# Hybrid decoder step: prompt attention in the block order 0, 1, 7, 6, 5, 4, 3, 2, with each selection mask made one block ahead

## The chip, the cores and the metric

The kernel runs on one core of a Trainium2 chip. The metric is the device time of one execution in microseconds, median of several runs.

## What is computed

One step of a two-layer decoder trunk (d = 1024) for a prompt of 1024 tokens and a sample group of 8 sequences of 4 tokens with 1024 tokens of past. Layer 0 is a recurrent mixer (RG-LRU and gated DeltaNet) with an MLP, layer 1 is sparse attention with an MLP. The change lies in the sparse attention of the prompt, in the reference:

```python
def blk(args):                      # one block of 128 queries
    q_b, qi_b, wi_b, bi = args
    tpos = bi * qb + jnp.arange(qb)
    sc = index_scores(qi_b, wi_b, ki)
    sc = jnp.where(kpos[None, None, :] <= tpos[None, :, None], sc, -jnp.inf)
    _, idx = lax.top_k(sc, topk)    # 256 keys for each query
    valid = idx <= tpos[None, :, None]
    return sparse_attend(q_b, k[bidx, idx], v[bidx, idx], valid)

o = lax.map(blk, (blocks(q), blocks(qi), blocks(wi), jnp.arange(nb)))   # 8 blocks
```

There are 8 query heads on 2 key heads. A block may only look back, so block i sees 128 (i + 1) keys; blocks 0 and 1 see at most 256 keys and need no selection. The blocks do not depend on each other.

## The kernel before

The program is written by hand, engine by engine, and the order of each engine is that of the code; semaphores join them. Selected keys are not gathered. Instead the index scores of blocks 2 to 7 and of the samples stay in SBUF (`sc`, `sc_s`), a bitwise search finds each row's 256th largest score, and a mask of 0 and -1e30 over all keys (`mb` for the prompt, `mb_s` for the samples) is added to the attention scores.

`mask(q)` (line 1156) makes one mask on VectorE in five instructions as wide as the block: equal to the limit, a running count of the equals, the equals that still fit into the quota, those above the limit, and the scaling to bf16 (lines 1160 to 1164). Each waits for the one before. Masks 0 to 5 belong to blocks 2 to 7 (384 to 1024 columns), mask 6 to the samples (32 partitions, 1056 columns). The last instruction counts up `mask_r`.

The prompt's attention goes over 16 groups, two for each block, one for each key head: group n has block n // 2. A group has four heads.

- PE, `scores(n)` (line 709): for each head the product of queries and keys, and a product of the identity with the mask that adds it in PSUM. There are two places in PSUM for heads, so the third head waits until the exponential of the first is done. A group of blocks 2 to 7 waits for its mask by `mask_r`.
- VectorE, `head_max` (line 1172): row maximum of each head (line 1169) and its scaling.
- ScalarE, `exps(n)` (line 927): exponentials of the four heads into `pr`, with the sums of the rows.
- VectorE, `normalise(n)` (line 1184): reciprocal and product, four times.
- PE, `values(n)` (line 738): for each tile of 128 keys four transposes (line 747) and, one tile later, the product with the values (line 753). Between them the transposed tile is copied to `ptt`: the first tile of a group by VectorE (line 1204), the others by ScalarE (`ptt_copies`, line 938).
- VectorE, `output(n)` (line 1179): copies the result of a group to `oq` (line 1182).

PE takes scores(n + 1) ahead of values(n). VectorE's loop over n is, in this order: the four maxima of group n + 1, the ptt copy of group n, the output of group n - 1, the normalising of group n + 1, and for n below 7 mask n. At n = 7 stands a copy of the sample queries (`qs`, line 1212), whose memory the masks use as scratch.

Behind the 16 groups comes the sample stage. SyncE loads the pages of past keys and values for it: the key pages of the first four sequences early, then (`rest_of_sync`, line 581) it waits for all seven masks and loads the value pages of sequences 0 and 1; the value pages of sequences 2 and 3 wait for the end of all 16 groups, and the rest follows as buffers come free.

Of the kernel before, what the change touches and what calls it, by code (L numbers as in the profile page):

```python
# [22 lines left out]
P = 128  # L23
# [7 lines left out]
QB = SEQ // P  # L31
# [18 lines left out]
KV = 2  # L50
# [135 lines left out]
def build(nc, A, O):  # L186

    ctx = ExitStack()
    with ctx:
# [321 lines left out]
        HEADS = GROUPS * GRP  # L511
        steps_before = [sum(k // KV + 1 for k in range(n)) for n in range(GROUPS + 1)]

# [85 lines left out]
        def rest_of_pe(pe, unit, first_unit, norm_sum, mlp):  # L599
# [110 lines left out]
            def scores(n):  # L710
                i, kv = n // KV, n % KV
                if i >= 2:
                    pe.wait_ge(S["mask_r"], i - 1)
                for g in range(GRP):
                    a = n * GRP + g
                    if a >= 2:
                        pe.wait_ge(S["at_exp"], a - 1)
                    for k, (c0, cn) in enumerate(cuts(P * (i + 1))):
                        bank = 2 * (a % 2) + k
                        pe.matmul(ps[:, bank, 0:cn], oq[:, GRP * kv + g, i * P:(i + 1) * P], oq[:, 8 + kv, c0:c0 + cn],  # L720
                                  start=True, stop=False, skip_group_check=True)
                        if i < 2:
                            mm = pe.matmul(ps[:, bank, i * P:(i + 1) * P], id_b[:, :], bias_b[:, :], start=False, stop=True,
                                           skip_group_check=True)
                        else:
                            mm = pe.matmul(ps[:, bank, 0:cn], id_b[:, :], mb[:, sc_off[i] + c0:sc_off[i] + c0 + cn],
                                           start=False, stop=True, skip_group_check=True)
                    mm.then_inc(S["at_mm"], 1)
# [9 lines left out]
            def values(n):  # L738
                i, kv = n // KV, n % KV
                pe.wait_ge(S["at_nrm"], GRP * (n + 1))  # L740
# [97 lines left out]
        def rest_of_act(act, own, norm_root, square_unit, mlp):  # L838
# [88 lines left out]
            def exps(n):  # L927
                w = P * (n // KV + 1)
                for g in range(GRP):
# [8 lines left out]
            def ptt_copies(n):  # L938
                for k in range(1, n // KV + 1):
                    c = steps_before[n] + k  # L940
                    act.wait_ge(S["at_tr"], c + 1)
                    if c >= 2:
                        act.wait_ge(S["at_pv"], c - 1)
                    act.activation(ptt[:, c % 2, :], ps[:, 4 + c % 2, :], ACT.Copy).then_inc(S["at_ptt"], 1)
# [52 lines left out]
        def rest_of_dve(dve, own, norm_mean, output_units, mlp):  # L997
# [157 lines left out]

            def mask(q):
                s, m, pn, w = rows_of[q]
# [6 lines left out]
                dve.tensor_scalar(m, pre, -1.0, -MASKED, ALU.add, ALU.mult).then_inc(S["mask_r"], 1)  # L1164
                dve.wait_ge(S["mask_r"], q + 1)

# [5 lines left out]
            def head_max(a):  # L1172
                if a < HEADS:
                    dve.wait_ge(S["at_mm"], a + 1)
                    if a >= 4:
                        dve.wait_ge(S["at_exp"], a - 3)
                    maximum(a, bank2(2 * (a % 2), P * (a // (GRP * KV) + 1)))

            def output(n):
                i, kv = n // KV, n % KV  # L1180
                dve.wait_ge(S["at_pv"], steps_before[n + 1])
                dve.tensor_copy(oq[:, GRP * kv:GRP * (kv + 1), i * P:(i + 1) * P], quad(6 + n % 2)).then_inc(S["at_o"], 1)

            def normalise(n):
                w = P * (n // KV + 1)
                for g in range(GRP):
# [9 lines left out]
            for n in range(GROUPS):  # L1196
# [10 lines left out]
                if n + 1 < GROUPS:  # L1207
                    normalise(n + 1)
                if n < NB:
                    mask(n)  # L1210
                if n == NB:
                    dve.tensor_copy(qs[:, :, :, :].rearrange("p b h t -> p h b t"),
# [1345 lines left out]
```

## Time and profile before

| | |
|---|---|
| median of 3 runs | 3252.92 us (3252.11 to 3254.89) |
| the profiled execution, its own time | 3254.98 us |
| its span | 3253.2 us |
| PE (matmul) busy | 2950.3 us, 91% |
| VectorE (DVE) busy | 1403.7 us, 43% |
| ScalarE (ACT) busy | 749.3 us, 23% |
| GpSimd (POOL) busy | 936.0 us, 29% |
| mean granted TensorE clock | 0.935 |

PE is TensorE's products, PEld its weight loads, SPq the DMA issues of SyncE. Times in the trace are microseconds from the start of the span. The granted clock is the share of TensorE's full clock (2.4 GHz) that the chip grants it; 0.5 is 1.2 GHz, and a value between the two is a mean over a stretch that had both. The 16 groups lie between some 1940 and 2189 us, the sample stage between 2189 and 2337 us; the MLPs of the two layers, which make up most of the span, lie in front and behind.

### The profile page before, as it was taken

The page shows a single profiled execution, that of the slowest core. Times are in us where ns is not written, and L with a number is a line of the kernel's source. Part 1 is how long each engine was busy: PE and PEld are TensorE (multiplying, and loading weights), DVE is VectorE, ACT ScalarE, POOL GpSimd, SP SyncE. Part 2 cuts the span into 40 slices and gives each one's busy share as a digit, 9 for nine tenths or more (in the row PEclk, how much of TensorE's full clock was granted, in tenths as well). Part 3 has the DMA queues.
Part 4 walks back from the last instruction along what each step waited for, and adds up shares of the span by engine and source line. Part 5 has one row for each costly group of instructions (what it writes and reads, how often), then busy time and mean ns, then how long its engine had stood idle before and what let it go on. Part 6 is the DMA issues. An engine that isn't in the chain of part 4 may idle for free.

```text
span 3253.2 us, 43038 instructions
## 1 busy us (share of the span) xinstructions
PE 2950.3 (91%) x17384; PEld 2735.1 (84%) x17393; DVE 1403.7 (43%) x1868; ACT 749.3 (23%) x1158; POOL 936.0 (29%) x561
## 2 busy tenths in 40 slices
PE   5989899978899999999989946898798999999996
PEld 5889779968899999999977933446698999999995
DVE  6568266653422222212568887531134222222225
ACT  3353323320200011100235552332202100001111
POOL 2334223303343333334321310000032344333331
PEclk8999989969999999999999967997699999999998
DMA  4112100012111111111311120003210111111111
GB/s 146 39 33 60 29 26 1 1 57 71 30 48 47 45 39 42 45 45 48 107 38 37 46 82 1 26 10 105 83 45 26 46 49 45 48 40 42 42 44 66
DMA packets 237233, 153.09 MB, mean 47 GB/s; under 512 B 21243, under 2 KB 232884, under 8 KB 236169
## 3 DMA queue, kind: packets, MB, share of 16 engines
q1 hardware_dynamic: 226000, 121.17, 13.1%
q10 hardware_dynamic: 11116, 30.33, 2.6%
q8 instruction: 77, 1.26, 0.2%
q14 instruction: 40, 0.33, 0.0%
HBM read 133.46 MB, written 18.01 MB: 47 GB/s over the span
## 4 chain that ended last, share of the span: by engine, by line
PE 78%; DVE 13%; ACT 6%; issue 1%; DMA 0%; ACTq 0%; DVEq 0%
PE ps L1435 59%; ACT junk L898 3%; PE ps L720 2%; PE ps L789 2%; PE ps L753 2%; PE ps L1602 1%; PE ps L1587 1%; PE ps L1606 1%; DVE hl L2512 1%; DVE uc L2165 1%; PE ps L822 1%; PE ps L1512 1%; DVE mx L1169 1%; PE ps L747 1%; DVE cnt L1124 1%
## 5 line engine op out<-in xcount | busy, mean ns | idle before, releaser
L1331 POOL TENSOR_TENSOR w_hi<-w_raw,ones 128x512 fp32r<-128x512 f32 (+1 forms) x250 | 373.5, 1494 | 2023.9 <-PE ps L1435 1908.9
L1435 PE MATMUL ps<-xh,w_hi 128*128 128x352 f32 x2928 | 645.6, 329 | 68.1 <-DVE xl L2463 23.4
L1435 PE MATMUL ps<-xl,w_hi 128*128 128x352 f32 x2928 | 636.3, 326 | 0.0
L1435 PE MATMUL ps<-xh,w_lo 128*128 128x352 f32 x2928 | 635.4, 325 | 0.0
L1435 PEld LDWEIGHTS ps<-xh,w_hi 128*128 128x128 f32 x2928 | 505.0, 191 | 76.8 <-issue 63.2
L1435 PEld LDWEIGHTS ps<-xh,w_lo 128*128 128x128 f32 x2928 | 507.3, 189 | 0.0
L1435 PEld LDWEIGHTS ps<-xl,w_hi 128*128 128x128 f32 x2928 | 503.0, 190 | 0.0
L1334 POOL TENSOR_TENSOR w_lo<-w_raw,w_hi 128x512 fp32r<-128x512 f32 (+1 forms) x250 | 491.9, 1968 | 19.6
L2528 DVE TENSOR_TENSOR x<-x,ps 128x1056 f32<-128x1056 f32 x128 | 160.6, 1254 | 502.0 <-PE ps L1435 502.0
L2063 ACT ACTIVATE hs<-hu 128x1056 f32<-128x1056 f32 x64 | 69.7, 1090 | 1253.4 <-DVE hu L2504 1253.4
L1435 PE MATMUL ps<-hh,w_hi 128*128 128x352 f32 x1536 | 333.2, 325 | 13.7 <-DVE hl L2512 13.7
L1435 PE MATMUL ps<-hh,w_lo 128*128 128x352 f32 x1536 | 331.1, 323 | 0.0
L1435 PE MATMUL ps<-hl,w_hi 128*128 128x352 f32 x1536 | 330.5, 323 | 0.0
L2504 DVE SCALAR_TENSOR_TENSOR hu<-ps,rstd 128x1056 f32<-128x1056 f32 x64 | 80.5, 1258 | 560.4 <-PE ps L1435 560.0
L1435 PEld LDWEIGHTS ps<-hh,w_hi 128*128 128x128 f32 x1536 | 260.9, 189 | 17.9 <-ACT hh L2065 17.9
L1435 PEld LDWEIGHTS ps<-hh,w_lo 128*128 128x128 f32 x1536 | 263.4, 188 | 0.0
L1435 PEld LDWEIGHTS ps<-hl,w_hi 128*128 128x128 f32 x1536 | 261.0, 188 | 0.0
L720 PE MATMUL ps<-oq 128*128 128x512 f32 (+3 forms) x192 | 91.1, 569 | 68.5 <-ACT pr L935 51.1
L720 PEld LDWEIGHTS ps<-oq 128*128 128x128 f32 x192 | 39.0, 223 | 104.2 <-ACT pr L935 60.8
L1368 POOL TENSOR_TENSOR dn_lo<-dn_lm,cst 128x512 f32<-128x512 f32 (+1 forms) x49 | 67.4, 1410 | 189.6 <-ACT dn_lm L1984 189.6
L2512 DVE TENSOR_TENSOR hl<-hs,hh 128x1056 fp32r<-128x1056 f32 x64 | 115.1, 1810 | 7.2 <-DVE hu L2504 4.2
L2165 DVE SCALAR_TENSOR_TENSOR uc<-ub,prm,uc 128x1080 f32<-128x1080 f32 x48 | 94.1, 1960 | 25.5 <-ACT uc L1813 24.3
(374 smaller groups left out, 3035.6 us busy)
## 6 DMA issues: line engine op xcount, KB each, us to landing
w_raw<-in_w_up SPq DMA_DIRECT2D x64, 512.0 KB, 4.1
w_raw<-in_w_down SPq DMA_DIRECT2D x128, 256.0 KB, 2.7
w_raw<-in_w_in_rec SPq DMA_DIRECT2D x24, 512.0 KB, 3.9
x_spill<-x ACTq DMA_DIRECT2D x2, 4224.0 KB, 12.8
x<-x_spill ACTq DMA_DIRECT2D x4, 2112.0 KB, 7.6
w_raw<-in_w_in_att SPq DMA_DIRECT2D x16, 512.0 KB, 3.8
kpg<-in_cache_k SPq DMA_DIRECT2D x64, 128.0 KB, 2.0
vpg<-in_cache_v SPq DMA_DIRECT2D x64, 128.0 KB, 2.0
```

Source lines behind the costliest of these rows:

```text
L720: pe.matmul(ps[:, bank, 0:cn], oq[:, GRP * kv + g, i * P:(i + 1) * P], oq[:, 8 + kv, c0:c0 + cn], start=True, stop=False, skip_group_check ...
L753: pe.matmul(ps[:, 6 + n % 2, :], vtok[:, k - 1, kv * P:(kv + 1) * P], ptt[:, (c - 1) % 2, :], start=k == 1, stop=k == i + 1).then_inc(S["a ...
L898: ins = act.activation(junk[0:pn, junk_off[q]:junk_off[q] + w], s, ACT.Sign, scale=-1.0, bias=trial[0:pn, q:q + 1].bitcast(F32), accum_out ...
L1331: pool.tensor_tensor(w_hi[:, j % 2, 0:n], w_raw[:, j % 2, 0:n], ones[:, 0:1].to_broadcast([P, n]), ALU.mult).then_inc(w_hi_done, 1)
L1334: pool.tensor_tensor(w_lo[:, j % 2, 0:n], w_raw[:, j % 2, 0:n], w_hi[:, j % 2, 0:n].bitcast(F32), ALU.subtract).then_inc(w_split, 1)
L1368: pool.tensor_tensor(dn[f"lo{l}"][c % 2][0:w, :, 0:w], dn["lm"][0:w, :, 0:w], cst[0:w, C_LEVEL + l:C_LEVEL + l + 1, 0:w].to_broadcast([w, ...
L1435: mm = pe.matmul(ps[:, 3 * (j % 2) + t, 0:n], w[:, j % 2, k * P:(k + 1) * P], r[:, k, c0:c0 + n], start=(k == 0 and p == 0), stop=(k == kt ...
L2063: act.activation(hs[:, q % 2, :], hu[:, q % 2, :], ACT.Square).then_inc(S["hsq_r"], 1)
L2165: ins = dve.scalar_tensor_tensor(uc[:, 0:UB - 3], ub[:, i:i + UB - 3], prm[:, at_w:at_w + 1], uc[:, 0:UB - 3], ALU.mult, ALU.add)
L2504: dve.scalar_tensor_tensor(hu[:, q % 2, :].rearrange("p (a t) -> p a t", a=3), set_view(first + q, 0, 3)[:, :, 0:352], 0.0, r3, ALU.max, A ...
L2512: dve.tensor_tensor(hl[:, q - 1, :], hs[:, (q - 1) % 2, :], hh[:, q - 1, :].bitcast(F32), ALU.subtract)\
L2528: dve.tensor_tensor(xm, xm, set_view(j, 0, 3)[:, :, 0:352], ALU.add).then_inc(set_free, 1)
```

## The change

A table `BLOCKS` gives the block of each pair of groups: 0, 1, 7, 6, 5, 4, 3, 2. All that depended on n // 2 as the block's number now asks `block_of(n)`: widths, offsets, and the count of tiles ahead of a group (`steps_before`). Masks are made in the order in which the blocks come (`MASKS`: 5, 4, 3, 2, 1, 0, then the samples), and `mask_after` says behind which n of VectorE's loop each stands: the mask of block 7 behind n = 0, then one behind the first group of each block for the block that follows, and the samples' behind n = 13. The copy of the sample queries moves from n = 7 to n = 14. Line numbers grow by 7 or 8 behind the table.

```diff
--- before.py
+++ after.py
@@ -509,7 +509,14 @@
         w_out_att = A["w_out_att"][0].rearrange("(k p) n -> p k n", p=P)
         GROUPS = QB * KV
         HEADS = GROUPS * GRP
-        steps_before = [sum(k // KV + 1 for k in range(n)) for n in range(GROUPS + 1)]
+        BLOCKS = [0, 1] + list(range(QB - 1, 1, -1))
+        MASKS = [i - 2 for i in BLOCKS[2:]] + [NB - 1]
+        mask_after = {0: 0, 4: 1, 6: 2, 8: 3, 10: 4, 12: 5, 13: 6}
+
+        def block_of(n):
+            return BLOCKS[n // KV]
+
+        steps_before = [sum(block_of(k) + 1 for k in range(n)) for n in range(GROUPS + 1)]
 
         def cuts(w):
             return [(c, min(512, w - c)) for c in range(0, w, 512)]
@@ -708,9 +715,9 @@
             pe.wait_ge(S["tk_act"], QB + 2)
 
             def scores(n):
-                i, kv = n // KV, n % KV
+                i, kv = block_of(n), n % KV
                 if i >= 2:
-                    pe.wait_ge(S["mask_r"], i - 1)
+                    pe.wait_ge(S["mask_r"], MASKS.index(i - 2) + 1)
                 for g in range(GRP):
                     a = n * GRP + g
                     if a >= 2:
@@ -736,7 +743,7 @@
                     pe.wait_ge(S["at_ptt"], c - n)
 
             def values(n):
-                i, kv = n // KV, n % KV
+                i, kv = block_of(n), n % KV
                 pe.wait_ge(S["at_nrm"], GRP * (n + 1))
                 for k in range(i + 2):
                     c = steps_before[n] + k
@@ -925,7 +932,7 @@
             token_stores()
 
             def exps(n):
-                w = P * (n // KV + 1)
+                w = P * (block_of(n) + 1)
                 for g in range(GRP):
                     a = n * GRP + g
                     act.wait_ge(S["at_max"], a + 1)
@@ -936,7 +943,7 @@
                                    accum_out=den[:, a % 8:a % 8 + 1]).then_inc(S["at_exp"], 1)
 
             def ptt_copies(n):
-                for k in range(1, n // KV + 1):
+                for k in range(1, block_of(n) + 1):
                     c = steps_before[n] + k
                     act.wait_ge(S["at_tr"], c + 1)
                     if c >= 2:
@@ -1153,7 +1160,8 @@
             own.then(dve.tensor_scalar(quota[:, :], cnt[:, :], -1.0, float(TOPK), ALU.mult, ALU.add))
             dve.wait_ge(S["kv_out"], 16 * 6)
 
-            def mask(q):
+            def mask(k):
+                q = MASKS[k]
                 s, m, pn, w = rows_of[q]
                 lim = cand[0:pn, q:q + 1].bitcast(F32)
                 eq, pre = scr[0][0:pn, 0:w], scr[1][0:pn, 0:w]
@@ -1162,7 +1170,7 @@
                 own.then(dve.scalar_tensor_tensor(eq, pre, quota[0:pn, q:q + 1], eq, ALU.is_le, ALU.mult))
                 own.then(dve.scalar_tensor_tensor(pre, s, lim, eq, ALU.is_gt, ALU.add))
                 dve.tensor_scalar(m, pre, -1.0, -MASKED, ALU.add, ALU.mult).then_inc(S["mask_r"], 1)
-                dve.wait_ge(S["mask_r"], q + 1)
+                dve.wait_ge(S["mask_r"], k + 1)
 
             def maximum(a, view):
                 col = mx[:, a % 4:a % 4 + 1]
@@ -1174,15 +1182,15 @@
                     dve.wait_ge(S["at_mm"], a + 1)
                     if a >= 4:
                         dve.wait_ge(S["at_exp"], a - 3)
-                    maximum(a, bank2(2 * (a % 2), P * (a // (GRP * KV) + 1)))
+                    maximum(a, bank2(2 * (a % 2), P * (block_of(a // GRP) + 1)))
 
             def output(n):
-                i, kv = n // KV, n % KV
+                i, kv = block_of(n), n % KV
                 dve.wait_ge(S["at_pv"], steps_before[n + 1])
                 dve.tensor_copy(oq[:, GRP * kv:GRP * (kv + 1), i * P:(i + 1) * P], quad(6 + n % 2)).then_inc(S["at_o"], 1)
 
             def normalise(n):
-                w = P * (n // KV + 1)
+                w = P * (block_of(n) + 1)
                 for g in range(GRP):
                     a = n * GRP + g
                     dve.wait_ge(S["at_exp"], a + 1)
@@ -1206,9 +1214,9 @@
                     output(n - 1)
                 if n + 1 < GROUPS:
                     normalise(n + 1)
-                if n < NB:
-                    mask(n)
-                if n == NB:
+                if n in mask_after:
+                    mask(mask_after[n])
+                if n == GROUPS - 2:
                     dve.tensor_copy(qs[:, :, :, :].rearrange("p b h t -> p h b t"),
                                     oq[:, 0:Q_HEADS, SEQ:TOK].rearrange("p h (b t) -> p h b t", t=DEC_SEQ))\
                         .then_inc(S["mask_r"], 1)
```

**VectorE, the mask of block 6.** `pr` are the probabilities that `normalise` scales, `scr` the scratch of the masks, `mx` the row maxima. Before, it stands behind n = 4, beside a group of block 2:

```order
L1189 RECIPROCAL rden<-den 128x1 [waits at_exp]
L1190 TENSOR_SCALAR pr_178<-pr_178,rden 128x384 [waits dve_chain]
L1160 TENSOR_SCALAR scr_142<-sc,cand 128x896
L1161 SCALAR_TENSOR_TENSOR scr_143<-ones,scr_142 128x896 [waits dve_chain]
L1162 SCALAR_TENSOR_TENSOR scr_142<-scr_143,quota,scr_142 128x896 [waits dve_chain]
L1163 SCALAR_TENSOR_TENSOR scr_143<-sc,cand,scr_142 128x896 [waits dve_chain]
L1164 TENSOR_SCALAR mb<-scr_143 128x896 [waits dve_chain]
L1169 TENSOR_REDUCE mx<-ps 128x1 [waits at_exp,at_mm,mask_r]
```

The first two rows are the last head of `normalise(5)`, the last one the first maximum of group 6. With the change, again behind n = 4:

```order
L1197 RECIPROCAL rden<-den 128x1 [waits at_exp]
L1198 TENSOR_SCALAR pr_178<-pr_178,rden 128x1024 [waits dve_chain]
L1168 TENSOR_SCALAR scr_142<-sc,cand 128x896
L1169 SCALAR_TENSOR_TENSOR scr_143<-ones,scr_142 128x896 [waits dve_chain]
L1170 SCALAR_TENSOR_TENSOR scr_142<-scr_143,quota,scr_142 128x896 [waits dve_chain]
L1171 SCALAR_TENSOR_TENSOR scr_143<-sc,cand,scr_142 128x896 [waits dve_chain]
L1172 TENSOR_SCALAR mb<-scr_143 128x896 [waits dve_chain]
L1177 TENSOR_REDUCE mx<-ps 128x1 [waits at_exp,at_mm,mask_r]
```

The mask is the same; the probabilities normalised in front of it are now those of block 7 (1024 columns) instead of block 2 (384).

**PE, the end of values(4) and the start of scores(6).** `oq` are queries and keys, `mb` the mask; the wait for `mask_r` is that for the mask. Before:

```order
L747 MATMUL ps<-ident,pr_169 128x128 x3
L753 MATMUL ps<-ptt,vtok 128x512 [waits at_ptt] x2
L720 MATMUL ps<-oq 128x512 [waits at_exp,mask_r]
L726 MATMUL ps<-mb,id_b 128x512
L720 MATMUL ps<-oq 128x512 [waits at_exp]
```

The two products with the values are the last of block 2. With the change:

```order
L754 MATMUL ps<-ident,pr_169 128x128 x3
L760 MATMUL ps<-ptt,vtok 128x512 [waits at_ptt] x2
L727 MATMUL ps<-oq 128x512 [waits at_exp,mask_r]
L733 MATMUL ps<-mb,id_b 128x512
L727 MATMUL ps<-oq 128x384
L733 MATMUL ps<-mb,id_b 128x384
L727 MATMUL ps<-oq 128x512 [waits at_exp]
```

Before, three tiles of values stand between these scores and those of the group in front, and the mask that they wait for (block 3, 512 columns) was made behind n = 1; now there are eight tiles, and the mask (block 6, 896 columns) is the one that VectorE makes meanwhile.

**VectorE, the samples' mask (`mb_s`).** Before, behind n = 6:

```order
L1190 TENSOR_SCALAR pr_178<-pr_178,rden 128x512 [waits dve_chain]
L1160 TENSOR_SCALAR scr_142<-sc_s,cand 32x1056
L1161 SCALAR_TENSOR_TENSOR scr_143<-ones,scr_142 32x1056 [waits dve_chain]
L1162 SCALAR_TENSOR_TENSOR scr_142<-scr_143,quota,scr_142 32x1056 [waits dve_chain]
L1163 SCALAR_TENSOR_TENSOR scr_143<-sc_s,cand,scr_142 32x1056 [waits dve_chain]
L1164 TENSOR_SCALAR mb_s<-scr_143 32x1056 [waits dve_chain]
L1169 TENSOR_REDUCE mx<-ps 128x1 [waits at_exp,at_mm,mask_r]
```

With the change, behind n = 13:

```order
L1198 TENSOR_SCALAR pr_169<-pr_169,rden 128x384 [waits dve_chain]
L1168 TENSOR_SCALAR scr_142<-sc_s,cand 32x1056
L1169 SCALAR_TENSOR_TENSOR scr_143<-ones,scr_142 32x1056 [waits dve_chain]
L1170 SCALAR_TENSOR_TENSOR scr_142<-scr_143,quota,scr_142 32x1056 [waits dve_chain]
L1171 SCALAR_TENSOR_TENSOR scr_143<-sc_s,cand,scr_142 32x1056 [waits dve_chain]
L1172 TENSOR_SCALAR mb_s<-scr_143 32x1056 [waits dve_chain]
L1177 TENSOR_REDUCE mx<-ps 128x1 [waits at_exp,at_mm,mask_r]
```

It has moved seven groups back, behind the normalising of block 2; only two groups follow it.

## Rows read from the trace of the kernel before

**Rows 1.** Windows: stretch, length, busy PE PEld DVE ACT POOL, clock, DMA.

```profile
1940.00:2047.00 107.00, 71.30 (x216) 38.74 (x218) 80.84 (x186) 27.45 (x79) 0.00 (x0) 0.76 0.05 15
2047.00:2177.00 130.00, 116.18 (x443) 61.06 (x450) 67.05 (x139) 53.86 (x98) 0.00 (x0) 1.00 0.04 12
```

**Rows 2.** Chain of waits around the mask of block 6: start, us, piece.

```profile
2000.67 2.04 DVE scr L1161
...
2007.51 2.08 PE ps L720 x2
```

**Rows 3.** Timeline of VectorE, groups with masks: start, us, instruction.

```profile
1948.78 0.69 DVE L1204 COPY ptt<-ps 128x512 f32<-128x512 f32 x1 [0.37 <-PE ps L747]
...
1950.96 0.42 DVE L1160 TENSOR_SCALAR scr<-sc,cand 128x384 f32<-128x384 f32 x1
...
1954.10 0.42 DVE L1169 TENSOR_REDUCE mx<-ps 128x1 f32<-128x256 f32 x1
...
1957.83 0.69 DVE L1204 COPY ptt<-ps 128x512 f32<-128x512 f32 x1 [0.24 <-PE ps L747]
...
2015.99 0.75 DVE L1160 TENSOR_SCALAR scr<-sc,cand 128x1024 f32<-128x1024 f32 x1
...
2022.46 0.69 DVE L1169 TENSOR_REDUCE mx<-ps 128x1 f32<-128x512 f32 x1
...
2029.30 0.69 DVE L1204 COPY ptt<-ps 128x512 f32<-128x512 f32 x1
...
2032.87 0.75 DVE L1160 TENSOR_SCALAR scr<-sc_s,cand 32x1056 f32<-32x1056 f32 x1
...
2039.45 0.82 DVE L1169 TENSOR_REDUCE mx<-ps 128x1 f32<-128x640 f32 x1
```

**Rows 4.** Timeline of VectorE, groups without masks (7 to 15).

```profile
2047.12 0.69 DVE L1204 COPY ptt<-ps 128x512 f32<-128x512 f32 x1
...
2053.99 0.83 DVE L1169 TENSOR_REDUCE mx<-ps 128x1 f32<-128x640 f32 x1 [2.74 <-PE ps L726]
...
2059.98 0.69 DVE L1204 COPY ptt<-ps 128x512 f32<-128x512 f32 x1
...
2125.99 0.69 DVE L1204 COPY ptt<-ps 128x512 f32<-128x512 f32 x1
...
2137.55 1.23 DVE L1169 TENSOR_REDUCE mx<-ps 128x1 f32<-128x1024 f32 x1 [7.10 <-PE ps L726]
...
2146.20 0.69 DVE L1204 COPY ptt<-ps 128x512 f32<-128x512 f32 x1
...
2150.18 0.76 DVE L1190 TENSOR_SCALAR pr<-pr,rden 128x1024 f32<-128x1024 f32 x1
...
2166.40 0.69 DVE L1204 COPY ptt<-ps 128x512 f32<-128x512 f32 x1
...
2177.55 0.69 DVE L1204 COPY ptt<-ps 128x512 f32<-128x512 f32 x1 [6.42 <-PE ps L747]
...
2188.26 0.69 DVE L1182 COPY oq<-ps 128x512 f32<-128x512 f32 x1 [9.42 <-PE ps L753]
```

**Rows 5.** Chain of waits within values(14), one of the repeated steps.

```profile
2170.93 0.44 PE ps L747 x4
2171.37 0.86 PE ps L753 x2
```

**Rows 6.** Windows: a stretch behind the mask of block 7, columns as in rows 1.

```profile
2020.00:2025.00 5.00, 0.79 (x1) 0.50 (x2) 3.98 (x7) 1.56 (x4) 0.00 (x0) 0.61 0.00 0
```

**Rows 7.** Timelines of SyncE's DMA issues and of PE, sample stage.

```profile
2040.18 17.15 SPq L551 DMA_DIRECT2D vpg<-in_cache_v  x16
...
2207.31 17.16 SPq L551 DMA_DIRECT2D kpg<-in_cache_k  x16
...
2224.75 2.58 PE L789 MATMUL ps<-pt_s,vpg 128*128 128x16 f32 x16 [0.36 <-ACT pt_s L960]
...
2241.61 3.77 PE L813 MATMUL ps<-ident,kpg 128*128 128x128 f32 x16
```

## The prediction

> **What bounds the kernel now.** I read the busy time by stretches first. The stretch up to 2047 us, in which all seven masks are made, has PE busy 71.30 of 107.00 us at a mean granted clock of 0.76 of full speed; the one behind it, which makes none, has 116.18 of 130.00 us at 1.00 [rows 1]. So the first stretch is where PE waits. The chain of waits says for what: it runs through the scan of a mask on VectorE (2.04 us) before it comes to the next score product on PE [rows 2]. The reason is the strict order on VectorE: the row maxima of the next group stand behind the mask, ScalarE's exponentials behind the maxima, and the third and fourth head on PE behind those. The blocks beside which masks are made now are the narrow ones, so PE has little to do meanwhile. Third, the timelines of VectorE give the price of each piece, and last I looked at the loads for the samples, which wait for the last mask.
>
> **How a group's time splits.** I measure from one ptt copy (line 1204) to the next; there are 16, one a group. Call period n the time from copy n to copy n+1. In it PE finishes values(n) and starts scores(n+2), and VectorE copies, normalises group n+1 and, where there is one, makes a mask; then come the maxima of group n+2. With v the block of group n and s that of group n+2:
>
> F(v,s), from the copy to the first maximum where no mask holds it up: 2053.99 - 2047.12 = 6.87 us for v=3, s=4, and 2137.55 - 2125.99 = 11.56 for v=6, s=7 [rows 4]. One more tile of values is 0.44 + 0.86 = 1.30 us on PE [rows 5], which leaves (4.69 - 3 x 1.30)/3 = 0.26 for one more tile of s. T(s), from the first maximum to the next copy: 5.99 for s=4 and 8.65 for s=7, so 0.89 a tile [rows 4]. The last two periods hold values alone: 11.15 and 10.71 us for block 7 [rows 4].
>
> VectorE's own time ahead of a mask, D, goes with the block of group n+1: 2032.87 - 2029.30 = 3.57 us for block 3 [rows 3] and 2150.18 + 0.76 - 2146.20 = 4.74 for block 7 [rows 4], 0.29 a block; 2.18 in period 0, which has no output copy [rows 3]. A mask M takes 3.14 us at 384 columns and 6.47 at 1024, so 0.67 for each 128 between them; the sample mask 6.58 [rows 3].
>
> The first maximum starts at the later of F and D + M. Below block 3 the formulas are an extrapolation, since every narrow period of the trace has a mask in it.
>
> **What a mask costs now.** In periods 0 to 6 the masks grow from 384 columns while F is 2.19, 2.19, 3.75, 3.75, 5.31, 5.31 and 6.87. D + M is 5.32, 6.80, 7.46, 8.42, 9.08, 10.04 and 10.15. The differences sum to 27.9 us. To this comes TensorE's clock: PE pauses behind its first two heads, the granted clock falls to a mean of 0.61 in the stretch from 2020 to 2025 [rows 6], which is part at 1.2 and part at 2.4 GHz, and the remaining heads run slowly. T is 6.84 us (2022.46 to 2029.30) where the formula gives 5.10 for block 3: 1.74 lost [rows 3]. In the five periods from 2 to 6 that makes 8.7.
>
> **The change, period by period.** The sets of v and of s over all groups are the same in both orders, and F and T are sums of a part in v and a part in s; so the plain work cancels and only what masks expose can differ. The new order of groups is blocks 0, 1, 7, 6, 5, 4, 3, 2, two groups each.
>
> Period 0 (mask of block 7): D + M = 2.18 + 6.47 = 8.65, then T 3.73 as measured there (1954.10 to 1957.83) [rows 3]: 12.4.
> Period 1 (no mask): D 3.0, T 3.7, and 1.0 that I add because PE has just paused and runs at 1.2 GHz: 7.7.
> Periods 2 and 3 (v=1, s=7): F 5.05 + T 8.65 = 13.7 each; in the first of them I add 1.7, one loss as above, while the clock rises: 29.1 together.
> Periods 4 and 5 (v=7, s=6): F 12.59; D + M in period 4 is 4.74 + 5.80 = 10.54, so the mask of block 6 is hidden by 2.0; T 7.77: 40.7.
> Periods 6 and 7 (v=6, s=5): F 11.03 against 9.59, hidden by 1.4; T 6.88: 35.8.
> Periods 8 and 9 (v=5, s=4): F 9.47 against 8.62, hidden by 0.8; T 5.99: 30.9.
> Periods 10 and 11 (v=4, s=3): F 7.91 against 7.67, hidden by 0.2; T 5.10: 26.0.
> Period 12 (v=3, s=2): F 6.35 against 3.57 + 3.14 = 6.71, 0.4 exposed; T 4.21: 10.9.
> Period 13, the sample mask: 3.28 + 6.58 = 9.86 against 6.35, 3.5 exposed; PE pauses as before, so T is 4.21 + 1.74: 15.8.
> Periods 14 and 15 (values of block 2, five tiles of 1.30 fewer each): 4.65 + 4.21 = 8.9.
>
> The sum is 218.2 us. Before, the same stretch runs from 1948.78 [rows 3] to the last output copy at 2188.26 [rows 4], 239.5. **The gain is 21.3 us.**
>
> **What is moved beside it.** The qs copy goes from period 7 to 14, behind the last normalise, where VectorE has 3.3 + 0.3 us of work against 4.65: nothing. The wait of SyncE for the last mask moves most. The 16 loads of v pages behind it take 17.15 us (from 2040.18 [rows 7]) and are now over long before they are used at 2224.75, in the sample stage, which begins as the stretch ends. After the change the mask is done 9.86 us into period 13, 14.8 before the stretch ends, so these loads end some 2.4 us behind the start of the sample stage; all later loads on that queue start at most 2.4 us late against it. The first of them with a consumer on PE is the k pages at 2207.31, used at 2241.61: of the 34 us between them 17.16 go into issuing the 16 loads, and the first 8 are needed first [rows 7]. Nothing for that, bounded by 0 and 2.4. Nothing else is added: 35 mask instructions, the score products and the copies are the same in number and shape.
>
> **A rule that speaks against it.** Without masks, at 2047 to 2177, the granted clock is 1.00 although PE pauses for the maxima in every period [rows 1]. The Trainium skill (TensorE: Matmul & The Clock Gate, "A second HAM failure mode: psum-queue depth-cycling") says that a PE that cycles through PSUM banks and idles shortly between groups of products can go back and forth between its two clocks. The trace disagrees with it for blocks 4 to 7; of blocks 3 and 2 without masks no row here shows anything. By it the narrow groups, now at the end, would still lose; that is the first rival.
>
> **Rivals.** First, the narrow tail runs at 1.2 GHz in part. Blocks 4 to 2 give PE short bursts, and so each of periods 10, 11 and 12 could lose 1.74 as in the masked periods, the values that follow another 1 each, and the opening of the sample stage some 4 (its transposes and scores twice as long for a few us). For it speaks that all narrow periods of the trace have a low clock [rows 1, 6]; against it, that all those have a pause made by a mask. Gain 21.3 - 8.2 - 4 = 9: 3244 us.
>
> Second, on the other side: masks take much longer beside wide groups. Today they run while ScalarE and PE mostly stand still; in periods 4 to 13 they run beside ScalarE's ptt copies and PE's products. If each took twice as long there, 3.8, 3.7, 3.6, 3.6, 3.1 and 6.6 us more would be exposed, 24.4 in all, and four more pauses would cost 1.74 each: 31.4, which gives 3263 us, slower by 10. It decides from a factor of about 1.7 on. Against it: the normalising products, which do run beside those copies, follow one line from block 3 to 7 [rows 3, 4].
>
> Third, the edit gains more than I count: no pause of period 0 or 13 lowers the clock, and the additions of 1.0, 1.7 and 1.7 vanish: 25.7, 3227 us. That the change does not do what it says I exclude, since the order of instructions has each mask directly behind the normalising of a wide group.
>
> **How the numbers follow.** The profiled execution took 3254.98 us, 2.06 above the median of the runs, 3252.92. Taken from its time the gain gives 3233.7, from the median 3231.6; I forecast **3232 us**. My own case (extrapolated narrow groups, phases of the clock in the sample stage, some 7 us either way) is 3225 to 3239 at 0.75; the first rival 0.13, the third 0.06, which partly overlaps; the second 0.04; late loads or something unseen 0.02. The range 3223 to 3243 leaves out the second rival and half of the first. A measurement of this kernel can tell 0.2%, 6.5 us, from no change: faster by more than that 0.92, within it 0.05, slower 0.03.
>
> **What would show it.** In the profile after, the first maximum of group 6 should start about 12.6 us behind ptt copy 4, with a pause of VectorE of some 2 us in front of it that ends on PE; the masks should be gone from the chain of waits but for those of blocks 7 and 3 and of the samples; the granted clock should be 1.00 from the first group of block 7 to that of block 3. The stretch should be near 218 us and the sample stage as long as now. The forecast is wrong if pauses on PE remain in periods 4 to 11, if the mask instructions are longer than now, or if PE in the sample stage waits for pages.

## The result and the profile after

Two slips of the part above first: `scores(n)` is line 710 of the kernel before, and SyncE's wait for all masks is its line 574.

| | before | after |
|---|---|---|
| median of the runs beside each other | 3253.9 us (3252.11 to 3254.97, 4 runs) | 3233.23 us (3231.53 to 3238.74, 4 runs) |
| the profiled execution, its own time | 3254.98 us | 3234.19 us |
| its span | 3253.2 us | 3232.4 us |
| the 16 groups, first ptt copy to last output copy | 239.48 us (from 1948.78) | 220.24 us (from 1947.41) |
| the sample stage, from there to the start of its last products | 145.97 us | 145.39 us |

The ratio is 0.994, with a 95% interval of 0.9923 to 0.9957; forecast were 3232 us. The spans differ by 20.8 us: the stretch gave 19.24, it began 1.37 earlier, the sample stage took 0.58 less, and what lies behind it 0.4 more. Only the first is clearly the change's own: in a second profile of the changed kernel the sample stage took 144.54 us, 0.85 less. The start of the stretch lay between 1945.18 and 1954.50 us over the executions profiled here, though the program in front of it is the same in all. One execution among all that were timed, of the second run of the masks one group earlier, took 11308.79 us; its ratio leaves it out, and its median, 3232.54 us, would be 3232.48 without it.

The windows of the kernel after, over the same stretches as before [rows 1], columns as there:

```profile
1940.00:2047.00 107.00, 89.96 (x315) 47.16 (x316) 71.86 (x154) 38.98 (x86) 0.00 (x0) 0.88 0.02 8
2047.00:2177.00 130.00, 108.68 (x447) 57.70 (x446) 76.87 (x168) 49.28 (x104) 0.00 (x0) 0.99 0.07 21
```

PE in the first stretch is busy for 89.96 us instead of 71.30, at a clock of 0.88 instead of 0.76; the second, which now holds the tail of the narrow groups and the first of the sample stage, stays at 0.99.

VectorE's timeline of the kernel after, groups 0 to 9 (start, us, instruction, idle time in front of it and what ended that):

```profile
1947.41 0.69 DVE L1212 COPY ptt<-ps 128x512 f32<-128x512 f32 x1 [0.37 <-PE ps L754]
...
1949.58 0.75 DVE L1168 TENSOR_SCALAR scr<-sc,cand 128x1024 f32<-128x1024 f32 x1
...
1956.06 0.43 DVE L1177 TENSOR_REDUCE mx<-ps 128x1 f32<-128x256 f32 x1
...
1960.61 0.69 DVE L1212 COPY ptt<-ps 128x512 f32<-128x512 f32 x1 [0.24 <-PE ps L754]
...
1995.53 0.69 DVE L1212 COPY ptt<-ps 128x512 f32<-128x512 f32 x1
...
2000.18 0.68 DVE L1168 TENSOR_SCALAR scr<-sc,cand 128x896 f32<-128x896 f32 x1
...
2005.33 0.63 DVE L1172 TENSOR_SCALAR mb<-scr 128x896 bf16<-128x896 f32 x1
2008.25 1.09 DVE L1177 TENSOR_REDUCE mx<-ps 128x1 f32<-128x896 f32 x1 [2.30 <-PE ps L733]
...
2015.99 0.69 DVE L1212 COPY ptt<-ps 128x512 f32<-128x512 f32 x1
...
2028.58 1.09 DVE L1177 TENSOR_REDUCE mx<-ps 128x1 f32<-128x896 f32 x1 [8.13 <-PE ps L733]
...
2036.32 0.69 DVE L1212 COPY ptt<-ps 128x512 f32<-128x512 f32 x1
...
2045.24 0.56 DVE L1172 TENSOR_SCALAR mb<-scr 128x768 bf16<-128x768 f32 x1
2047.83 0.96 DVE L1177 TENSOR_REDUCE mx<-ps 128x1 f32<-128x768 f32 x1 [2.03 <-PE ps L733]
...
2054.67 0.69 DVE L1212 COPY ptt<-ps 128x512 f32<-128x512 f32 x1
...
2065.69 0.96 DVE L1177 TENSOR_REDUCE mx<-ps 128x1 f32<-128x768 f32 x1 [6.83 <-PE ps L733]
```

These are the counterparts of [rows 3, 4]: a ptt copy begins a period, an L1177 behind a mask or an idle time is the first maximum. Period 0 makes the mask of block 7 and goes from 1947.41 to 1960.61, 13.20 us. Period 4 makes that of block 6, from 2000.18 to 2005.96, and the first maximum follows 12.72 us behind the copy at 1995.53. Its twin without a mask, period 5, has 2028.58 - 2015.99 = 12.59. In period 6 the first maximum comes 11.51 us behind the copy at 2036.32, in its twin 2065.69 - 2054.67 = 11.02. So the pair that should have been alike differs by 0.49 us.

The sixteen periods, in us:

| period | forecast | measured |
|---|---|---|
| 0 (mask of block 7) | 12.4 | 13.20 |
| 1 | 7.7 | 7.49 |
| 2, 3 | 29.1 | 13.62 + 13.81 |
| 4 (mask of block 6), 5 | 40.7 | 20.46 + 20.33 |
| 6 (block 5), 7 | 35.8 | 18.35 + 17.86 |
| 8 (block 4), 9 | 30.9 | 16.30 + 15.45 |
| 10 (block 3), 11 | 26.0 | 14.11 + 12.89 |
| 12 (block 2) | 10.9 | 12.01 |
| 13 (samples) | 15.8 | 15.48 |
| 14, 15 | 8.9 | 4.66 + 4.22 |
| sum | 218.2 | 220.24 |

The chain of waits of the kernel after at the mask of block 5 (start, us, piece), which answers to [rows 2]:

```profile
2045.24 0.57 DVE mb L1172
2045.86 1.12 PE ps L727 x2
2047.20 0.43 PE ps L727 x2
2047.83 0.97 DVE mx L1177
```

A mask that I had hidden by 1.4 us stands in the chain. PE waits for it itself. PE's timeline of the kernel after, the first score products of blocks 5, 4, 3 and 2, and the third head's in period 13:

```profile
2045.86 1.12 PE L727 MATMUL ps<-oq 128*128 128x512 f32 x2 [0.17 <-DVE mb L1172]
...
2081.13 1.13 PE L727 MATMUL ps<-oq 128*128 128x512 f32 x2 [0.53 <-DVE mb L1172]
...
2111.95 1.13 PE L727 MATMUL ps<-oq 128*128 128x512 f32 x2 [0.89 <-DVE mb L1172]
...
2138.02 0.91 PE L727 MATMUL ps<-oq 128*128 128x384 f32 x2 [1.26 <-DVE mb L1172]
...
2154.68 1.65 PE L727 MATMUL ps<-oq 128*128 128x384 f32 x2 [4.30 <-ACT pr L942]
```

In periods 6, 8, 10 and 12 PE stands still for 0.17, 0.53, 0.89 and 1.26 us in front of them. The last row is the stop for the samples' mask, as before the change: ScalarE's exponential, and with it the third head, waits for the maxima behind that mask on VectorE.

### The profile page after: what moved, and what is told of

Read it like the earlier page. It is cut to its first block, busy times and chain, and to the rows that moved or that the text cites. A ratio compares the mean times of both kernels' runs of the same rounds, so it can differ in the third digit from the quotient of the medians.

```text
span 3232.4 us, 43047 instructions
## 1 busy us (share of the span) xinstructions
PE 2941.3 (91%) x17393; PEld 2730.7 (84%) x17393; DVE 1405.3 (43%) x1868; ACT 748.1 (23%) x1158; POOL 935.6 (29%) x561
## 3 DMA queue, kind: packets, MB, share of 16 engines
q8 instruction: 77, 1.26, 0.2%
## 4 chain that ended last, share of the span: by engine, by line
PE 78%; DVE 13%; ACT 6%; issue 1%; DMA 0%; DVEq 0%; ACTq 0%
PE ps L1443 60%; ACT junk L905 3%; PE ps L727 2%; PE ps L796 2%; PE ps L1610 1%; PE ps L1595 1%; PE ps L760 1%; PE ps L1614 1%; DVE hl L2520 1%; DVE uc L2173 1%; PE ps L1520 1%; PE ps L829 1%; DVE mx L1177 1%; DVE cnt L1131 1%; DVE hu L2512 1%
## 5 line engine op out<-in xcount | busy, mean ns | idle before, releaser
L1443 PE MATMUL ps<-hh,w_hi 128*128 128x352 f32 x1536 | 333.2, 325 | 13.7 <-DVE hl L2520 13.7
L1443 PEld LDWEIGHTS ps<-hh,w_hi 128*128 128x128 f32 x1536 | 260.8, 189 | 17.9 <-ACT hh L2073 17.9
L2173 DVE SCALAR_TENSOR_TENSOR uc<-ub,prm,uc 128x1080 f32<-128x1080 f32 x48 | 94.1, 1960 | 25.5 <-ACT uc L1821 24.3
```

The source lines that it names most:

```text
L1443: mm = pe.matmul(ps[:, 3 * (j % 2) + t, 0:n], w[:, j % 2, k * P:(k + 1) * P], r[:, k, c0:c0 + n], start=(k == 0 and p == 0), stop=(k == kt ...
L2173: ins = dve.scalar_tensor_tensor(uc[:, 0:UB - 3], ub[:, i:i + UB - 3], prm[:, at_w:at_w + 1], uc[:, 0:UB - 3], ALU.mult, ALU.add)
```

## The experiments

Two questions were open: whether the place of the masks or the order of the blocks brings the gain, and why periods 6, 8, 10 and 12 are longer than their twins. For the second my theory was that PE's first score product waits for a mask that was made in the same period, so that this head's product is to be added to the mask's end; the rival was that a mask and PE's or ScalarE's work slow each other down. Each diff is against the changed kernel; each ratio is to the kernel before.

**The old order, masks beside the block in front.**

```diff
-        BLOCKS = [0, 1] + list(range(QB - 1, 1, -1))
+        BLOCKS = list(range(QB))
-        mask_after = {0: 0, 4: 1, 6: 2, 8: 3, 10: 4, 12: 5, 13: 6}
+        mask_after = {1: 0, 4: 1, 6: 2, 8: 3, 10: 4, 12: 5, 13: 6}
```

> Blocks in the old order 0 to 7, but each mask made beside the first group of the block in front of its own (behind n = 1, 4, 6, 8, 10, 12; the samples' behind n = 13). Theory 'place': what counts is that a mask has values on PE beside it, not which block comes first. From the rows of the changed kernel a group whose mask is just made starts its first maximum at D + M + H, with H from 1.49 us (512 columns) to 2.57 (1024) for the first head; the periods add up to about 220 us, the same as with the new order, so 3231 to 3236 us. Rival 'order': the gain comes from the wide blocks being first; then this order gives back most of it, 3245 to 3254 us.

Measured: 3238.22 us (5 runs), ratio 0.9948 (0.9935 to 0.9962). The stretch took 226.20 us, so the place of the masks alone brings 13.3 of the 19.2 us and the order the other 5.9. The time lies between the ranges of the two theories; neither holds alone. The stretch was 6 us longer than I expected. By the formulas of the prediction with H added, periods 4, 6 and 8 (masks of blocks 3, 4 and 5) would take 13.7, 15.8 and 17.9 us; they took 14.56, 18.50 and 19.45, which is 5.1 of the 6. The period of the mask of block 4 shows why. VectorE's timeline in this kernel:

```profile
2020.37 0.49 DVE L1172 TENSOR_SCALAR mb<-scr 128x640 bf16<-128x640 f32 x1
...
2024.04 0.82 DVE L1177 TENSOR_REDUCE mx<-ps 128x1 f32<-128x640 f32 x1 [3.18 <-PE ps L733]
```

Its PE timeline and two of its windows at the same place:

```profile
2020.91 2.08 PE L727 MATMUL ps<-oq 128*128 128x512 f32 x2 [2.59 <-DVE mb L1172]
```

```profile
2015.00:2020.00 5.00, 3.32 (x12) 1.31 (x10) 4.82 (x9) 1.19 (x2) 0.00 (x0) 1.00 0.00 0
2020.00:2025.00 5.00, 3.87 (x7) 2.06 (x9) 1.75 (x4) 0.00 (x0) 0.00 (x0) 0.53 0.00 0
```

PE stands still for 2.59 us until the mask is done. Up to then the granted clock was 1.00, behind it 0.53, that is nearly all at 1.2 GHz, and the pair of score products takes 2.08 us. From the end of the mask to the first maximum it takes 3.18 us; the same mask in the changed kernel takes 1.76. So in the old order a narrow group stands in front of each wider mask: PE runs out of work, and behind the longer stops what follows runs slowly. In front of blocks 3 to 7 PE stands still for 2.96, 2.59, 2.23, 1.86 and 1.50 us here; the clock was 1.00 in front of each stop, 0.66, 0.53 and 0.73 behind the first three (1995 to 2000, 2020 to 2025 and 2053 to 2056 us), and 1.00 behind the last two. That is the clock term of the prediction, in another order.

**The new order, masks early.**

```diff
-        mask_after = {0: 0, 4: 1, 6: 2, 8: 3, 10: 4, 12: 5, 13: 6}
+        mask_after = {0: 0, 1: 1, 2: 2, 3: 3, 4: 4, 5: 5, 6: 6}
```

> The new block order, but the seven masks made one after the other behind n = 0 to 6, as before the change. Theory 'place': masks 2 to 4 in the order of the table now stand beside blocks 0 and 1 and are exposed (6.6, 3.1 and 4.2 us), those behind n = 4 to 6 are hidden; the stretch is about 228 us, the time 3238 to 3244 us. Rival 'order': the same as the changed kernel, 3231 to 3235 us.

Measured: 3242.76 us, ratio 0.9963 (0.9951 to 0.9975). The stretch took 228.36 us, 11.1 less than before; 228 was expected. Periods 1 (13.41 us), 2 (18.52) and 3 (20.27) pay, where the changed kernel has 7.49, 13.62 and 13.81: 5.9, 4.9 and 6.5 us, where 6.6, 3.1 and 4.2 were expected. Part of that is slow clock again, since T is 10.34 and 11.15 us in periods 2 and 3 instead of 8.65. So the total agrees better than its terms, 17.3 against 13.9, and that is in part luck. VectorE's timeline in period 2 of this kernel:

```profile
1971.79 0.69 DVE L1212 COPY ptt<-ps 128x512 f32<-128x512 f32 x1 [0.24 <-PE ps L754]
...
1974.83 0.61 DVE L1168 TENSOR_SCALAR scr<-sc,cand 128x768 f32<-128x768 f32 x1
...
1979.97 1.23 DVE L1177 TENSOR_REDUCE mx<-ps 128x1 f32<-128x1024 f32 x1
...
1990.31 0.69 DVE L1212 COPY ptt<-ps 128x512 f32<-128x512 f32 x1
```

The mask stands in front of the first maximum, which follows it with no idle time. Place and order brought 13.3 and 11.1 us alone and 19.2 together: part of what both take away is the same exposed work, so they do not add up.

**Each hidden mask one group earlier.**

```diff
-        mask_after = {0: 0, 4: 1, 6: 2, 8: 3, 10: 4, 12: 5, 13: 6}
+        mask_after = {0: 0, 4: 1, 5: 2, 7: 3, 9: 4, 11: 5, 13: 6}
```

> The changed kernel, with the masks of blocks 5, 4, 3 and 2 made behind n = 5, 7, 9 and 11 instead of 6, 8, 10 and 12, one group earlier. Theory 'awaited': in the changed kernel PE's first score product waits for the mask that has just been made, which lengthens periods 6, 8, 10 and 12 by 0.5, 0.85, 1.2 and 1.6 us; here these four periods get as long as their twins without a mask (17.86, 15.45, 12.89 and about 10.6), 4.1 us less in all, about 3229 us. Rival 'contention': those periods are longer because a mask and PE's work slow each other; then the length moves to periods 5, 7, 9 and 11 and the stretch stays at 220 us.

Measured: 3228.75 us, ratio 0.992 (0.9906 to 0.9933), stretch 216.94 us. The same masks now run beside groups of the same or a greater width, one period in front of their use. Periods 6 to 12 are 17.86, 17.92, 15.45, 15.51, 12.89, 12.95 and 10.43 us: the even ones, now without masks, lost 0.49, 0.85, 1.22 and 1.58, and the odd ones with them gained no more than 0.06. If a mask slowed other work down, or the reverse, the odd ones would have grown by what the even ones lost. The rival falls. VectorE's timeline in this kernel:

```profile
2023.76 0.56 DVE L1172 TENSOR_SCALAR mb<-scr 128x768 bf16<-128x768 f32 x1
2027.48 1.09 DVE L1177 TENSOR_REDUCE mx<-ps 128x1 f32<-128x896 f32 x1 [3.16 <-PE ps L733]
...
2035.22 0.69 DVE L1212 COPY ptt<-ps 128x512 f32<-128x512 f32 x1
...
2046.25 0.96 DVE L1177 TENSOR_REDUCE mx<-ps 128x1 f32<-128x768 f32 x1 [6.57 <-PE ps L733]
```

The mask of block 5 is over before the maximum of another group, and VectorE still idles 3.16 us there. The first maximum of block 5 then comes 11.03 us behind the copy, as in the twin. The chain of waits there has no mask:

```profile
2042.78 1.81 PE ps L760 x4
2044.59 0.86 PE ps L727 x2
2046.25 0.97 DVE mx L1177
```

From 2044.59, where PE is through with the products in front, to the maximum it takes 1.66 us, against 2045.86 to 2047.83 = 1.97 in the changed kernel. The 0.49 us of its period 6 are thus 0.17 of standing still and some 0.3 by which the first head takes longer behind the wait. The three other masks agree: 0.85, 1.22 and 1.58 lost are 0.53, 0.89 and 1.26 of standing still and 0.32 or 0.33 more each time. Part of this can be seen in the weight loads of PE for that product, first in this kernel, then in the changed one:

```profile
2044.00 0.19 PEld L727 LDWEIGHTS ps<-oq 128*128 128x128 f32 x1 [0.24 <-issue]
```

```profile
2045.85 0.30 PEld L727 LDWEIGHTS ps<-oq 128*128 128x128 f32 x2 [0.99 <-DVE mb L1172]
```

In this kernel the first load stands beside the products of the group in front, 0.6 us before they end; in the changed kernel the load waits for the mask too, and starts 0.01 us ahead of its own product. In `scores(n)` the wait for the mask stands in front of the product of queries and keys, which does not read the mask; only the product behind it (L733) does. To move the wait there is another way to these 4.1 us, which was not tried.

**One mask a group, the samples' among wide groups.**

```diff
-        MASKS = [i - 2 for i in BLOCKS[2:]] + [NB - 1]
-        mask_after = {0: 0, 4: 1, 6: 2, 8: 3, 10: 4, 12: 5, 13: 6}
+        MASKS = [5, 4, 3, 2, NB - 1, 1, 0]
+        mask_after = {0: 0, 4: 1, 5: 2, 6: 3, 7: 4, 8: 5, 9: 6}
```

> The changed kernel, with one mask behind each of n = 0 and n = 4 to 9, the samples' fifth of the last six (behind n = 7). Theory: nothing waits for a mask but in periods 0 and 4; besides the 4.1 us of the four awaited masks the pause of 3.5 us in period 13 goes and with it 1.4 us of slow clock behind it, so the stretch is 211 us and the time 3223 to 3227 us. If the loads of the value pages mattered, the sample stage would be shorter than 145 us too; I expect no change there, although they start some 50 us earlier.

Measured: 3228.98 us, ratio 0.9923 (0.9909 to 0.9936), stretch 211.18 us where 211 was expected. Periods 10 to 13 are 12.89, 12.90, 10.42 and 10.43: the 5 us of the samples' mask in period 13 are gone. Yet the median stayed at that of the run before it. The sample stage took 146.97 us here and 145.0 there. PE's timeline at its first products with the values, and windows there, first of the kernel before this one, then of this:

```profile
2198.72 2.68 PE L796 MATMUL ps<-pt_s,vpg 128*128 128x16 f32 x16 [0.36 <-ACT pt_s L967]
...
2195.00:2200.00 5.00, 1.55 (x12) 1.38 (x12) 1.78 (x7) 3.14 (x9) 0.00 (x0) 0.98 0.39 114
2200.00:2205.00 5.00, 5.00 (x24) 4.92 (x24) 0.00 (x0) 0.00 (x0) 0.00 (x0) 0.50 0.27 80
```

```profile
2196.04 3.60 PE L796 MATMUL ps<-pt_s,vpg 128*128 128x16 f32 x16 [0.36 <-ACT pt_s L967]
...
2195.00:2200.00 5.00, 4.33 (x19) 4.03 (x19) 1.13 (x4) 0.92 (x3) 0.00 (x0) 0.50 0.16 49
```

The same sixteen products take 3.60 us at a granted clock of 0.50, and 2.68 in the kernel before, where the clock falls to 0.50 while they run (a mean of 0.69 from 2198.72 to 2201.40). That is 0.9 of the 2 us by which the sample stage is longer; 1.5 lie ahead of these products and 0.45 are won back behind them. The spans of the two profiled executions differ by 2.6 us (3227.0 and 3224.4): of the 5.8 us of the stretch, 2 went into the sample stage and 1.6 into a later start, and 0.4 were won behind the stage. Why the medians agreed is not seen from two profiles; that is why both kernels were run again below.

**The first mask cut up.** On top of the edit above, the five instructions of the mask of block 7 stand in the gaps of groups 0 to 3 instead of in a row:

```diff
-        mask_after = {0: 0, 4: 1, 5: 2, 6: 3, 7: 4, 8: 5, 9: 6}
+        mask_after = {4: 1, 5: 2, 6: 3, 7: 4, 8: 5, 9: 6}
...
+                if a == 2:
+                    first_mask(0)
...
+                    if g == 2 and n in (1, 2):
+                        first_mask(2 * n)
...
+                if n < 2:
+                    first_mask(2 * n + 1)
```

`first_mask(step)` issues the instruction with that number of `mask(0)`: the first goes between the maxima of group 0, where VectorE idles for PE, the second and fourth behind the normalising in periods 0 and 1, the third and fifth ahead of the third maximum of groups 2 and 3.

> The version with one mask per group, and besides its first mask (block 7) cut into its five instructions, each put where VectorE waits or nearly waits: one in front of the third maximum of group 0, the scan behind n = 0, one in front of the third maximum of group 2, one behind n = 1, the last in front of the third maximum of group 3. Periods 0 and 1 take 13.21 and 7.33 us where the mask stands in one piece. Theory: only what exceeds F (3.82 us at 1.2 GHz) is exposed, 2.18 + 2.36 = 4.54 and 3.04 + 1.32 = 4.36, so the two take about 8.4 and 8.1, 4 us less together, and the stretch is 207 us. Rival: the pieces only push the maxima behind them, and the two periods stay at 20.5 us together. On the whole time 4 us is near what five runs can tell.

Measured: 3221.45 us (4 runs), ratio 0.9897 (0.9882 to 0.9911): the fastest version here, 12.6 us below the 3234.07 of the changed kernel that was run beside it (below). The stretch took 207.16 us, periods 0 and 1 together 16.06 instead of 20.5. VectorE's timeline in periods 0 and 1:

```profile
1949.37 0.69 DVE L1233 COPY ptt<-ps 128x512 f32<-128x512 f32 x1 [0.37 <-PE ps L754]
...
1951.55 2.28 DVE L1183 TENSOR_TENSOR_SCAN scr<-ones,scr 128x1024 f32<-128x1024 f32 x1
...
1954.93 1.27 DVE L1185 SCALAR_TENSOR_TENSOR scr<-scr,quota,scr 128x1024 f32<-128x1024 f32 x1
...
1957.31 0.68 DVE L1233 COPY ptt<-ps 128x512 f32<-128x512 f32 x1
...
1960.35 1.28 DVE L1187 SCALAR_TENSOR_TENSOR scr<-sc,cand,scr 128x1024 f32<-128x1024 f32 x1
```

Each piece takes as long as in one row, but most of it lies where VectorE idled before: the first maxima come 4.50 and 4.35 us behind the copies, where a mask in one piece has 8.66 in period 0 and period 1 without a mask has 3.82. Period 2 gives back 0.4 of the gain (14.07 us instead of 13.63). The sample stage took 143.3 us, the shortest here; why was not tried.

**Three runs again,** for the size of the differences between executions: the one with a mask a group, the one with each mask one group earlier, and the change itself.

> The kernel with one mask per group once more, beside the other versions on the same chip. In the traces its stretch is 5.8 us shorter than that of the version one group earlier, but the medians were the same (3228.98 and 3228.75). Theory: the stretch is the same in every execution and the rest (the recurrent layer in front, the clock in the sample stage) varies by some us, so the stretch comes out at 211.2 again and the median some 4 us below the next one's. Rival: a shorter stretch is given back by a longer sample stage (147.0 against 145.0 us in the two profiles) in every execution; then the medians are the same again.

> The kernel with four masks one group earlier once more, for the same comparison: stretch 216.9 us, sample stage 145 to 147 us, median 3227 to 3231 us.

> The changed kernel once more, for the same comparison: stretch 220.2 us, sample stage 145 to 147 us, median 3231 to 3235 us.

Measured: 3227.14 us (ratio 0.9917, 0.9904 to 0.993), 3232.54 (0.9932, 0.9919 to 0.9945) and 3234.07 (0.9937, 0.9924 to 0.995), the stretches 211.26, 216.34 and 220.52 us, the sample stages 147.03, 145.49 and 144.54. The theory of the first expectation is borne out: the first median lies 5.4 us below the second, for 5.1 us of stretch. Of its rival this much is true, that the sample stage of a mask a group is again some 1.5 us longer than that of the kernel compared with it. The second median lies above the range that was expected. So a stretch comes back within 0.6 us, while the median of one edit moved by 3.8 us between two sets of runs, which were on two chips. Within this set, with the mask cut up as its first, the medians lie 5.7, 5.4 and 1.5 us apart for 4.1, 5.1 and 4.2 us of stretch. A difference of 4 us between two edits is told apart by the stretch, not by the medians.

## Why the prediction was right

**The split of a period.** Right. Periods without a mask, 5, 7 and 9, measured 20.33, 17.86 and 15.45 us against 20.36, 17.91 and 15.46 by the formulas; their extrapolation to blocks 3 and 2, which no row of before showed, gives 13.01 for period 11 against 12.89. Periods 14 and 15 took 8.88 against 8.9.

**Which masks are hidden.** This is the step that failed: "The first maximum starts at the later of F and D + M." It holds only where the group's scores do not need that mask. In the kernel before, a mask stood in front of a maximum on VectorE, but belonged to a later group. After the change the maximum's own scores wait for it, and the first head's product, H, comes behind: 2.30 us from the mask's end for block 6, then 2.03, 1.76, 1.49 and 1.22 for block 2. Set against F, D + M + H exposes the masks that I took for hidden by 1.4, 0.8 and 0.2 us by 0.6, 0.9 and 1.3, and that of block 2 by 1.6 instead of 0.4; measured against the periods without them were 0.49, 0.85, 1.22 and 1.58. Periods 6 to 12 together took 3.4 us more than the sum had. The run with the masks one group earlier won these back. The prediction had named the sign of being wrong here, "if pauses on PE remain in periods 4 to 11": they remained, in front of the scores of 6, 8 and 10.

**The terms for the clock.** The 1.7 us in period 2 did not occur: 13.62 against 13.7 without it. Period 1 took 7.49, so 0.8 of the 1.0 that I added. Period 13, 9.89 + 5.59, bears out the pause there: 1.5 more than the T of 4.10 in period 12. Period 0 was 0.8 too short in the sum, because T took 4.55 instead of 3.73: the 3.73 had been measured at a clock of 0.72 and 0.62 (1950 to 1955 and 1955 to 1960 us before), and here it was 0.50 from 1950 to 1960. Windows of the kernel after at its start, in the first wide groups and in the tail:

```profile
1950.00:1955.00 5.00, 2.25 (x7) 1.19 (x5) 4.89 (x4) 0.00 (x0) 0.00 (x0) 0.50 0.00 0
...
1970.00:1975.00 5.00, 5.00 (x15) 1.97 (x13) 2.53 (x7) 0.48 (x1) 0.00 (x0) 1.00 0.00 0
...
2135.00:2140.00 5.00, 3.65 (x10) 1.14 (x8) 3.60 (x8) 0.61 (x2) 0.00 (x0) 1.00 0.00 0
...
2155.00:2160.00 5.00, 4.33 (x15) 2.39 (x15) 2.58 (x7) 2.09 (x7) 0.00 (x0) 0.73 0.41 115
```

The clock is 1.00 as soon as the first wide group comes. The errors in single periods partly cancel: +3.4 in periods 6 to 12, +0.8 in period 0, -1.7 in periods 2 and 3, and -0.5 in periods 1 and 13 with the rest, together the 2.0 us between 218.2 and 220.24. The forecast was nearer in the time than in its parts.

**The first rival, a slow tail.** It did not come. From 1970 to 2150 us every window of 5 us has a clock of 1.00, blocks 4, 3 and 2 among them, though PE pauses in each of these periods (by up to 1.34 us); 1.2 GHz returns only with the stop for the samples' mask, 0.93 from 2150 and 0.73 from 2155 on. The Trainium skill (TensorE: Matmul & The Clock Gate, "A second HAM failure mode: psum-queue depth-cycling") says that short idle times between groups of products, with PSUM banks taken in turn, make the clock go back and forth. This trace disagrees with it, at 1.00 throughout. The 12 us of this rival were not lost. Where the clock did drop, a longer stop stood in front: 2.96, 2.59 and 2.23 us in the old order, and 4.30 here, in front of PE's product at 2154.68.

**The second rival, longer masks beside wide groups.** The mask of block 6 takes from 2000.18 to 2005.96, 5.78 us beside a group of block 7, and 5.80 were forecast from the trace of before. It falls.

**The loads.** Right at nothing. SyncE's timeline of the kernel after, the value pages and the key pages behind them:

```profile
2153.90 35.43 SPq L558 DMA_DIRECT2D vpg<-in_cache_v  x32
...
2190.11 17.16 SPq L558 DMA_DIRECT2D kpg<-in_cache_k  x16
```

The value pages are issued at 2153.90 instead of 2040.18 [rows 7]. The key pages behind them start 22.5 us after the end of the stretch instead of 19.1, so 3.4 us late where the prediction had at most 2.4; it cost nothing that shows. With a mask a group they went out at 2095.70, and the sample stage was no shorter (146.97 us). In the waits of PE from 2160 to 2325 us no load appears; the largest is for `pt_s` of ScalarE, 9.4 us in three.

## What to carry to other kernels

A wait that is taken off an engine's queue can come back as a wait of the work itself: when something is made just in time for its first user, the user's own start-up counts behind it, and one group of slack cost nothing here, where the timeline had idle time. Work in a strict order is best put in the gaps that the engine has anyway, cut up if need be: cutting up one mask brought 4.0 us here. And before a small edit is judged by medians, compare the stretch it acts on: it came back within 0.6 us here, while the median of one edit moved by 3.8 from one chip to another.

## What the runs showed of the hardware

- The granted clock stayed at 1.00 through 180 us of groups in which PE stood still often but never for more than 1.34 us at a time; in the old order it was 0.66, 0.53 and 0.73 behind stops of 2.96, 2.59 and 2.23 us, and 1.00 behind stops of 1.86 and 1.50.
- The first head of scores took 0.32 us more behind a wait than behind running work, whether PE stood for 0.17 us or for 1.26; its weight load started 0.01 us ahead of the product behind the wait, and beside earlier products without it.
- A busy PE is not always granted the full clock: with the masks one group earlier PE stood still for 3.12 us up to 2198.09, the clock fell while it worked again, and from 2200 to 2205 us PE was busy for 5.00 of 5.00 us at 0.50.
- The sample stage, whose program was not touched, took between 143.3 and 147.0 us; two profiles of one kernel differed by 0.1 to 0.9 us.
